# A two-layer hybrid trunk on one core: VectorE's S5 matrices, top-k rounds and index dots set in a new order

## The reference

```python
for l in range(DEPTH):                                  # DEPTH = 2
    h = rmsnorm(x, norm_mix[l]);  proj = h @ w_in[l]
    y_a = s5_mixer(u, ...)        # 16 groups, 64 complex states each, a linear recurrence over the 1024 tokens, then a GLU
    y_b = dsa_attention(dq, dk, dv, iq, ik, iw, rel_bias)
    y_c = retention(rq, rk, rv, rg, ret_gn[l])          # 4 heads, chunks of 128
    x = x + concatenate([y_a, y_b, y_c]) @ w_out[l]
    x = x + (silu(gate) * up) @ w_ffn_out[l]            # d_ff = 2816
# inside dsa_attention, per block of 128 queries:
score = einsum(relu(iq . ik), iw);  score = where(causal, score, NEG_INF)
_, sel = top_k(score, 256)                              # 256 keys per query
p = softmax(q . k[sel] * scale + bias);  y = p @ v[sel]
```

## Time and profile before

| | |
|---|---|
| median of 3 runs | 2772.22 us (2771.98 to 2778.08) |
| the profiled execution | 2779.92 us |
| its span, first to last instruction | 2777.6 us |
| PE busy | 2591.4 us, 93% |
| DVE busy | 1568.5 us, 56% |
| POOL busy | 1312.8 us, 47% |
| ACT busy | 1013.2 us, 36% |
| mean granted TensorE clock | 0.968 |

### The profile page before, as it was taken

The page is one execution under the profiler, slowest core; times in us unless marked ns, Lnnn a source line. Parts: engine busy times, 40 slices in busy tenths (PEclk is TensorE's granted clock), DMA queues, the critical chain, the costliest instruction groups (busy, mean ns, idle before and its releaser), DMA issues. The chain is left out here.

```text
span 2777.6 us, 34714 instructions
## 1 busy us (share of the span) xinstructions
PE 2591.4 (93%) x13515; PEld 2035.0 (73%) x13515; DVE 1568.5 (56%) x2785; ACT 1013.2 (36%) x1472; POOL 1312.8 (47%) x818
## 2 busy tenths in 40 slices
PE   8798787989999999999999989989999999999998
PEld 6566655767777777778777767766777778888887
DVE  4859666778999224666232375477999942221111
ACT  5222144425343533323344422342434354322222
POOL 3332144435463475445555522443645356655655
PEclk9988899999999999999999999999999999999999
DMA  5232012222222144223222241221222224333332
GB/s 159 69 121 57 26 37 84 69 61 73 72 76 70 55 148 124 84 65 99 87 81 81 80 122 54 69 61 54 84 63 80 63 62 146 119 99 106 101 107 88
DMA packets 385665, 232.90 MB, mean 84 GB/s; under 512 B 29592, under 2 KB 371552, under 8 KB 383072
## 3 DMA queue, kind: packets, MB, share of 16 engines
q1 hardware_dynamic: 385136, 229.62, 27.9%
q10 hardware_dynamic: 368, 1.08, 0.1%
HBM read 213.88 MB, written 14.69 MB: 82 GB/s over the span
## 5 line engine op out<-in xcount | busy, mean ns | idle before, releaser
L681 POOL TENSOR_TENSOR w_lo<-w_raw,w_hi 128x1024 fp32r<-128x1024 f32 (+2 forms) x408 | 902.3, 2212 | 1322.4 <-ACT w_hi L792 1322.3
L1693 PE MATMUL psum<-h_hi,w_hi 128*128 128x512 f32 x1984 | 800.8, 404 | 17.4 <-ACT h_hi L816 7.1
L792 ACT ACTIVATE w_hi<-w_raw 128x1024 fp32r<-128x1024 f32 (+2 forms) x408 | 397.4, 974 | 1107.1 <-PE psum L1693 1070.9
L1693 PE MATMUL psum<-h_lo,w_hi 128*128 128x512 f32 x1984 | 770.1, 395 | 0.9 <-POOL h_lo L689 0.9
L1693 PE MATMUL psum<-h_hi,w_lo 128*128 128x512 f32 x1984 | 514.6, 390 | 0.0
L1693 PEld LDWEIGHTS psum<-h_hi,w_hi 128*128 128x128 f32 x1984 | 378.7, 191 | 130.1 <-issue 37.1
L1693 PEld LDWEIGHTS psum<-h_lo,w_hi 128*128 128x128 f32 x1984 | 378.2, 191 | 80.2 <-issue 1.9
L1693 PEld LDWEIGHTS psum<-h_hi,w_lo 128*128 128x128 f32 x1984 | 373.6, 188 | 76.7
L1313 DVE MAX8 top<-scores 128x8 f32<-128x512 f32 (+5 forms) x384 | 341.8, 890 | 8.1
L1315 DVE MATCH_REPLACE8 scores<-top,scores 128x512 f32<-128x512 f32 (+5 forms) x384 | 336.3, 876 | 0.0
L1693 PE MATMUL psum<-a_hi,w_hi 128*128 128x512 f32 x704 | 284.7, 404 | 18.3 <-DVE xs L1136 11.1
(11 more groups left out here) (296 smaller groups left out, 2945.4 us busy)
## 6 DMA issues: line engine op xcount, KB each, us to landing
w_raw<-in_w_ffn_in_dram SPq DMA_DIRECT2D x176, 512.0 KB, 3.8
w_raw<-in_w_ffn_out_dram SPq DMA_DIRECT2D x96, 384.0 KB, 3.1
w_raw<-in_w_in_dram SPq DMA_DIRECT2D x68, 512.0 KB, 3.8
w_raw<-in_w_out_dram SPq DMA_DIRECT2D x32, 512.0 KB, 3.6
x_half<-xs SPq DMA_DIRECT2D x8, 1024.0 KB, 6.8
xs<-x_half SPq DMA_DIRECT2D x8, 1024.0 KB, 6.9
w_raw<-in_w_ffn_out_dram SPq DMA_DIRECT2D x32, 256.0 KB, 2.6
out_dram<-mixed SPq DMA_DIRECT2D x8, 512.0 KB, 3.4
```

The lines of the kernel that those rows point to most:

```text
L681: eng.tensor_tensor(w_lo(u, n), w_raw[:, u % 3, 0:n], w_hi[:, u % 2, 0:n].bitcast(F32), ALU.subtract).then_inc(sems["weights_ready"], 1)
L792: act(w_hi[:, u % 2, 0:n], w_raw[:, u % 3, 0:n], ACTF.Copy).then_inc(sems["hi_ready"], 1)
L1693: return eng.matmul(out_, lhsT, rhs, start=start, stop=stop, skip_group_check=True)
```

## The change

1. **Block 2 drops instead of picks.** Of 384 keys 256 are kept, so 128 are dropped. The last score step of block 2 writes a negated and reversed copy, `flipped`; 16 rounds take its 128 largest, and the mask is then made where the marker stands. Block 2 has 16 rounds, all other blocks 32 (`BLOCK_ROUNDS`). Eight rounds of block 3 move from proj(0,1) into proj(0,0).
2. **S5 matrices as steps of their own.** Six `s5_prep` steps make Z of the first half (0, 1), E of the first half (2, 3) and Z of the second half (4, 5). In layer 0 they stand between the retention steps of proj(0,1), in layer 1 at units 1 to 3 of proj(1,1). To lie beside retention they work in `prep_tmp` (area) rather than in scratch, and the two Z buffers change places. The `s5` steps keep the rest.
3. **Index-dot steps one unit apart.** In proj(0,0) they alternate with units and with `s5_set`; in mixout(l,0) one step of scores follows each unit from 1 to 6, the two first with a retention step, the last three with two rounds of block 4 each. The rest of `late` lies in ffn(l,0).

```diff
+BLOCK_ROUNDS = [max(0, min(n - TOPK, TOPK)) // 8 for n in NK]
-    return 1.0 if step[0] in ("dma", "diag") else 5.0
+    return {"dma": 1.0, "diag": 1.0, "s5_prep": 3.0, "scores": 7.0}.get(step[0], 5.0)
...
-    out += weave(main[5:8], [("s5_set", 0, s) for s in range(5)])
     sc = score_steps(0, 0)
-    out += weave(main[8:15], sc[:3] + blend(rounds(2), sc[3:]))
+    out += main[5:6] + [("s5_set", 0, 0), ("s5_set", 0, 1)]
+    for n in range(3):
+        out += main[6 + n:7 + n] + [sc[n], ("s5_set", 0, 2 + n)]
+    out += weave(main[9:15], rounds(2, 0, 4) + sc[3:4] + rounds(2, 4, 10) + sc[4:] + rounds(2, 10) + rounds(3, 0, 8))
...
-    out += weave(main[:14], blend(retention_steps(0, 0, 3) + s5, rounds(3, 0, 16)), 0)
+    ret = blend(retention_steps(0, 0, 3), [("s5_prep", 0, n) for n in range(6)])
+    out += weave(main[:14], blend(ret + s5, rounds(3, 8, 16)), 0)
...
     def late(l):
         sc = score_steps(l, 1)
-        side = sc[:3] + blend(retention_steps(l, 1, 0, 2) + sc[3:] + retention_steps(l, 1, 2), rounds(4))
+        ret = retention_steps(l, 1)
+        lead = [[], [sc[0], ret[0]], [sc[1], ret[1]], sc[2:3]]
+        lead += [sc[n:n + 1] + rounds(4, 2 * n - 6, 2 * n - 4) for n in range(3, 6)]
+        side = blend(sc[6:] + ret[2:], rounds(4, 6))
...
-    out += weave(main[1:N_PROJ], [("s5", 1, s) for s in range(16)], 0, 15)
+    out += weave(main[1:N_PROJ], [("s5_prep", 1, n) for n in range(6)] + [("s5", 1, s) for s in range(16)], 0, 15)
...
+                    if b == 2:
+                        link(ts(flipped, score[b][:, ::-1], -1.0, None, MUL))
...
-                if r == ROUNDS - 1:
-                    ts(score[b], score[b], TAKEN, MASKED, ALU.not_equal, MUL).then_inc(sems["mask_ready"], 1)
+                if r == BLOCK_ROUNDS[b] - 1:
+                    if b == 2:
+                        ins = ts(score[b], flipped[:, ::-1], TAKEN, MASKED, ALU.is_equal, MUL)
+                    else:
+                        ins = ts(score[b], score[b], TAKEN, MASKED, ALU.not_equal, MUL)
+                    ins.then_inc(sems["mask_ready"], 1)
...
+            def s5_prep(l, n):
+
+                if n == 0 and l == 0:
+                    eng.wait_ge(sems["x1_stored"], 16)
+                if n < 2:
+                    inputs(0, n)
+                elif n == 2:
+                    first_rotation()
+                    rotations(0, 0, 5, prep_tmp)
+                elif n == 3:
+                    rotations(0, 5, 7, prep_tmp)
+                else:
+                    inputs(1, n - 4)
```

More of the change, by code:

```diff
@@ L98, in blend, with rounds @@
     return out + others[n:]
-def rounds(b, first=0, last=ROUNDS):
-    return [("round", b, r) for r in range(first, last)]
+def rounds(b, first=0, last=None):
+    return [("round", b, r) for r in range(first, BLOCK_ROUNDS[b] if last is None else last)]
 def retention_steps(l, h, first=0, last=15):
@@ L183, in mix_and_ffn @@
         return got
-    out += [("fillmix", 0, 0, counter[0])] + mix_and_ffn(0, 0, late(0))
+    out += [("fillmix", 0, 0, counter[0])] + mix_and_ffn(0, 0, *late(0))
     main = window("mixout", 0, 1)
@@ L1513, in s5_set, with first_rotation, rotations @@
                     link(tt(s5_bb[:, 1, :, :], s5_t[:, 0, :, :], s5_t[:, 1, :, :], ADD))
+            zs, ys = [P, 8, 4, 16], [P, 4, 4, 32]
+            pw = [s5p[:, o:o + 9, :] for o in (PR, PI)]
+            def first_rotation():
+                eng.memset(Et[:, 0, :, 0:1], 1.0)
+                link(eng.memset(Et[:, 1, :, 0:1], 0.0))
+            def rotations(hh, first, last, place):
+                qs = slice(4 * hh, 4 * hh + 4)
+                for k in range(first, last):
+                    n = 1 << k
+                    sh = [P, 4, n]
+                    rr, ri = (s5p[:, o + k, qs].unsqueeze(2).broadcast_to(sh) for o in (RR, RI))
+                    t_ = [place[:, i // 2, (i % 2) * 256:(i % 2) * 256 + 4 * n].rearrange("p (q c) -> p q c", q=4)
+                          for i in range(4)]
+                    cmul(Et[:, 0, :, n:2 * n], Et[:, 1, :, n:2 * n], Et[:, 0, :, 0:n], Et[:, 1, :, 0:n],
+                         rr, ri, *t_)
@@ new lines, in inputs @@
+            def inputs(g, c):
+                za, zb = (prep_tmp[:, i, :].rearrange("p (m q e) -> p m q e", m=8, q=4) for i in range(2))
+                of_g = slice(4 * g, 4 * g + 4)
+                pr, pi = (pw[i][:, 0:8, of_g].unsqueeze(3).broadcast_to(zs) for i in range(2))
+                tt(za, pr, s5_bb[:, c, of_g, :].unsqueeze(1).broadcast_to(zs), MUL)
+                link(tt(zb, pi, s5_bb[:, 1 - c, of_g, :].unsqueeze(1).broadcast_to(zs), MUL))
+                for half in range(2):
+                    rows_ = slice(64 * half, 64 * half + 64)
+                    other = slice(16 * (1 - half), 16 * (1 - half) + 16)
+                    eng.memset(Z[g][rows_, c, :, :, other], 0.0)
+                    ins = tt(Z[g][rows_, c, :, :, 16 * half:16 * half + 16], za[rows_], zb[rows_], ADD if c else SUB)
+                if c:
+                    ins.then_inc(sems["z_ready"], 1)
+                    eng.wait_ge(sems["z_ready"], st.add("z_ready"))
+                else:
+                    link(ins)
@@ L1536, in outputs @@
                     link(tt(yb, power(1, sl, ys), ni_, MUL))
[L1537 removed]
+                    flat = [Z[hh][:, c, 4 * m:4 * m + 4, :, :].rearrange("p m q e -> p (m q e)") for c in range(2)]
                     link(tt(flat[0], fa, fb, ADD))
@@ L1665, in _ @@
                     s5_set(*step[1:])
+                elif what == "s5_prep":
+                    s5_prep(*step[1:])
                 elif what == "s5":
```

81 lines of the change are left out of this document (24 added, 57 removed).

## The result

The changed kernel took 2762.0 us (2759.7 to 2762.45, 5 runs), the kernel before beside it 2776.9: a ratio of 0.9948, interval 0.9934 to 0.9963, some 14.5 us off. The forecast was 30. The direction was right, the size twice too large. (That 2762.0 lies inside the range given with the forecast, 2727 to 2764, is no merit: it reached far enough up for half the gain.)

The account below looks back on a forecast made before the run. PE, busy 93% of the span, was taken as the bound, time counting when it idles or runs at the lower clock. 7 + 6 + 12 + 12 - 3 - 3 = 31, said 30, from 2772.2 gave 2742 us; range 2727 to 2764.

Parts of the forecast that it names:

- the mixouts: mixout(0,0) and mixout(1,0): 12 us off each, 9 of waits for relu and additions and 3 of clock.
- the COPY's wait: proj(0,0): PE waits about 9 us for the COPY of the retention banks, in front of unit 10.
- the turn's wait in proj(0,1): PE's wait in front of retention's last turn grows from 4.2 by 11 to about 15 us.
- the two S5 outputs: proj(0,1): the wait at the first falls from 10.99 us to 0, at the second from 5.96 to about 5.
- proj(1,1) at nothing: proj(1,1): no net change; waits of 17 to 18 us against 14.6, one low-clock stretch less; bounds 5 won, 8 lost.
- The ffns behind them: 3 us back each: ffn(l,0): 7.5 us of DVE work moves in, half taken as waits, 3 us lost each; bounds 0 and 7.5.
- The ffns give back most: Rival: exps slipping make ffn waits 15 us a layer instead of 3, 2766, or 2754 with one layer's worth; chance 0.15.
- proj(0,0): 7 us off: proj(0,0): fewer DVE rounds, less those moved in, net 7.2 us; waits for additions go, 2 to 4 return at rotation.
- What counts then is DVE's sum up to retention's rotation: proj(0,0): 19.9 us of rounds less, 12.1 of block 3 more, flip 0.5, odds 0.1; net 7.2 off.
- proj(0,1): 6 us off: proj(0,1): waits and additions of 23 us against 28, first output 2 shorter at full clock; bounds 8 lost, 10 won.
- 7.7 above the median: Whole kernel before: the profiled execution, 2779.9 us, taken as 7.7 above the runs' median, so the forecast started from 2772.2.
- Slower: Rival: in ffn(l,0) DVE runs out of idle and exps come late: 2818, or 2783 in the last quarter alone; chance 0.04.

Follow-up runs that it names:

- e3: The changed kernel with no rounds among the steps of retention's group norm in the ffns (20 of block 4 ahead, 6 behind retention): 2742.9 us, 0.9884.
- e2: The changed kernel with the last dot step of block 3 four rounds later in proj(0,0): 2753.1 us, 0.9924.
- e8: The changed kernel with proj(0,0)'s four rounds ahead of the COPY set behind it and 14 rounds between block 3's additions: 2752.5 us, 0.9916.
- e7: The changed kernel with proj(0,0) set as before: s5_set at units 5 to 7, block 2's dots behind, its 16 rounds woven, then eight of block 3: 2757.8 us, 0.993.
- e6: The kernel before with the second edit alone (S5 preparation as steps of their own, both layers): 2774.1 us, 0.9987.
- e5: The changed kernel with all six preparation steps of layer 0 among retention's chunk steps, none among its group norm: 2745.7 us, 0.9892.
- e14: The changed kernel once more, unaltered, for a second profile: 2762.1 us, 0.9949.

## Why the forecast was off

Right: the mixouts, mechanism and size. Without the dot step that moved into the ffn they gave 12.0 and 13.6 us where 12 was forecast, 8.5 and 8.4 of it waits (9 forecast) and 3.5 and 5.2 clock (3 forecast). Right too are the COPY's wait (9, 8.60); the turn's wait in proj(0,1) (15, 13.74) and the two S5 outputs (0 and 5, measured 0 and 6.63); proj(1,1) at nothing, within 2 us.

Wrong, in order of size:

1. **"The ffns behind them: 3 us back each".** The stages gave back 5.4 and 9.9 in the first profiles, 12.1 and 8.7 in the second. The step that failed is where the loss would be paid: forecast were waits at the exps, and no clock. The exps' waits fell; new ones of 4.16 and 4.65 came up close to each other at the group norm, where rounds per retention step had grown, with the clock at 0.50 behind each. The 2.9 us by which the waits of each stage grew match the 3 by luck, as a balance of other terms. On top came the clock (1.5 and 5.9, then 8.4 and 3.8) and 1.2 of the moved dot step. e3 moved the rounds and had 7.1 and 8.4 back. The time that came out is near the rival "The ffns give back most" with one layer's worth, but not by its mechanism: the exps waited 12.9 us, not more than 14.7.
2. **"proj(0,0): 7 us off", in its step "What counts then is DVE's sum up to retention's rotation".** The rule is right (e2, e8, e7), the sum lacked two terms: the 4.96 us in which DVE itself waits for a relu behind ACT's weight split, and the first rotation operation held by POOL, 3.08 for 1.22. With 7.2 - 5.0 - 1.9 little is left, and the rotation turn, 2 us earlier, then ran at 1.2 GHz. Measured 0.8 more in the first profiles, 1.0 less in the second ones. e2 takes the relu's wait away and gets 5.3 us of waits back.
3. **"proj(0,1): 6 us off"** was too small: 10.3 and 9.1 measured. The waits came as added up (4.9, where 28 less 23 was forecast), but 5.7 and 4.4 less were lost to the clock, where I had put 2. In the first trace of before the clock was at 1.2 GHz from 273 to 294 us but for 3.4 us of it, around the 10.99 of the earlier trace rows; that went with the wait. The reason given for the waits fails: by e6 the preparation alone saves none, it exchanges the 10.99 for the turn's, and the 4.9 come only when eight rounds of block 3 also leave the stage. No run moved these rounds out without the preparation.
4. The profiled execution of before was set 7.7 above the median. In five more sets of runs the median of before was 2775 to 2778, so it was only 2 to 5; that moves the forecast of the time and not the 30.

Two sums of the forecast don't come out: the terms named for proj(1,1) give about 16, not 17 to 18 (16.3 and 14.6 were measured), and a quarter of the 82 us of the rival "Slower" is about 20, which gives 2757 with its 6 taken off, not 2783.

On the lock the forecast had cited the Trainium skill, page "SBUF — State Buffer", section "SBUF: two separate sides", for a hold that lasts the whole instruction. The traces agree: all 63 held operations lie beside a POOL operation, and in the pair shown halving POOL's instruction nearly halves the hold, 2.31 to 1.28 us. By the second profiles the shortfall, 31 less 14.5, is 6 in proj(0,0), 15 in the two ffns and 3 in stages put at nothing, less 3 in proj(0,1) and 4 in the mixouts. What decides in which execution a stretch at 1.2 GHz follows a short wait stays open.

## What to carry to other kernels

Where an engine is a queue in order, sum it up to each point where PE waits, and put into the sum what the engine itself waits for: a small operation on ACT may stand behind one that waits for PE. Keep filler (rounds, preparation) away from chains that go back and forth between engines, such as a group norm, and put it where the trace shows that engine idle: e3 and e5 did that alone and took 18 and 15 us. Compare kernels by PE's waits, stage by stage, and count time at the lower clock only where PE is not waiting, or it is counted twice. Expect more than a wait's own length from taking a long one away.

## What was not expected of the hardware

- PE's waits in a stage repeat within 2 us, the clock's loss less well: 10.5 to 14.9 us in ffn(0,0) in six profiles with 32.2 to 32.9 of waits (after, e2, e5, e7, e8, e14), and single executions of the kernel before from 2765.7 to 2785.4 us.
- Waits of 16.4 us in a stage almost wholly at the full clock made it 21.4 us longer.
- A DVE tensor-tensor operation on two SBUF operands beside a POOL one on SBUF is held until the POOL instruction ends: 2.31 us beside 1024 columns, 1.28 beside 512, while an unheld one of its kind takes 0.28.
